# Queries and keys of the block attention as tokens by channels, normed along the row on DVE and turned by PE afterwards

## The reference, cut to what matters

```python
h = rms_norm(x, norm_mix_g[i])
z = h @ w_in[i]
z_glu, gq, gk, gv, gr, ga, mq, mk, mv = jnp.split(z, offsets, axis=-1)
y_a = conformer_conv_branch(z_glu, ...)      # gate, 31 tap convolution, layer norm, silu
y_b = gla_branch(gq, gk, gv, gr, ga, ...)    # gated linear attention, 4 heads
y_c = moba_branch(mq, mk, mv, ...)           # 8 heads of 128 channels

# in moba_branch
q = rms_norm(q.reshape(b_sz, s, MOBA_HEADS, MOBA_HD), q_norm_g).transpose(0, 2, 1, 3)
k = rms_norm(k.reshape(b_sz, s, MOBA_HEADS, MOBA_HD), k_norm_g).transpose(0, 2, 1, 3)
...
s_own = jnp.einsum('bhqd,bhkd->bhqk', qc, k_own).astype(jnp.float32) * scale
```

## Time and profile before

| | us |
|---|---|
| median of 3 runs | 1613.31 (1612.99 to 1614.22) |
| profiled execution, whole | 1614.08 |
| its span, first to last instruction | 1612.0 |
| PE busy | 1596.1 (99%) |
| PE weight loads busy | 1383.0 (86%) |
| DVE busy | 1044.7 (65%) |
| ACT busy | 774.5 (48%) |
| POOL busy | 32.3 (2%) |
| mean granted clock of PE | 0.997 |
| DMA | 297 MB, 184 GB/s |

### The profile page before, as it was taken

The page is one execution under the profiler, slowest core; times in us unless marked ns, Lnnn a source line. Parts: engine busy times, 40 slices in busy tenths (PEclk is TensorE's granted clock), DMA queues, the critical chain, the costliest instruction groups (busy, mean ns, idle before and its releaser), DMA issues.

```text
span 1612.0 us, 23109 instructions
## 1 busy us (share of the span) xinstructions
PE 1596.1 (99%) x8642; PEld 1383.0 (86%) x8642; DVE 1044.7 (65%) x1215; ACT 774.5 (48%) x899; POOL 32.3 (2%) x52
## 2 busy tenths in 40 slices
PE   8999999999999999999999999999999999999998
PEld 7989998888888888888888888888888888888886
DVE  6598655665667646655477777765447777765554
ACT  6444434444555444444455555543345555544543
POOL 5000000000000000000000000000000000000000
PEclk9999999999999999999999999999999999999999
DMA  7666555555655566565566666565665666656564
GB/s 236 178 181 175 165 160 160 172 182 166 196 181 178 184 208 194 184 192 185 162 178 192 189 193 187 182 200 193 191 193 171 194 191 189 193 183 196 175 204 144
DMA packets 155959, 297.23 MB, mean 184 GB/s; under 512 B 9559, under 2 KB 11955, under 8 KB 155888
## 3 DMA queue, kind: packets, MB, share of 16 engines
q1 hardware_dynamic: 155376, 296.00, 59.7%
q0 software_dynamic: 480, 0.25, 0.1%
q10 hardware_dynamic: 32, 0.01, 0.0%
HBM read 294.12 MB, written 2.10 MB: 184 GB/s over the span
## 4 chain that ended last, share of the span: by engine, by line
PE 97%; DVE 1%; DMA 1%; ACT 1%; issue 0%; POOL 0%; SPq 0%; DVEq 0%; ACTq 0%
PE psum L482 20%; PE psum L498 17%; PE psum L500 17%; PE psum L499 17%; PE psum L485 10%; PE psum L461 4%; PE psum L462 4%; PE psum L463 4%; PE psum L578 1%; PE psum L515 1%; PE psum L623 0%; PE psum L532 0%; DMA out<-fin 0%; DVE w_lo L1102 0%; ACT junk L839 0%; DMA xtok<-in_x 0%
## 5 line engine op out<-in xcount | busy, mean ns | idle before, releaser
L1102 DVE TENSOR_TENSOR w_lo<-raw,w_hi 128x1024 fp32r<-128x1024 f32 x550 | 670.2, 1223 | 484.2 <-ACT w_hi L822 483.8
L822 ACT CAST w_hi<-raw 128x1024 fp32r<-128x1024 f32 x550 | 575.4, 1050 | 671.8 <-PE psum L500 409.8
L482 PE MATMUL psum<-h_both,w_hi 128*128 128x512 f32 x1408 | 353.8, 393 | 0.0
L482 PEld LDWEIGHTS psum<-h_both,w_hi 128*128 128x128 f32 x1408 | 254.2, 190 | 45.6
L498 PE MATMUL psum<-w_hi,h_both 128*128 128x512 f32 x608 | 240.5, 396 | 0.4 <-DVE w_lo L1102 0.4
L500 PE MATMUL psum<-w_hi,h_both 128*128 128x512 f32 x608 | 236.9, 390 | 0.0
L499 PE MATMUL psum<-w_lo,h_both 128*128 128x512 f32 x608 | 236.8, 389 | 0.0
L485 PEld LDWEIGHTS psum<-h_both,w_lo 128*128 128x128 f32 x1408 | 192.1, 190 | 13.7
L485 PE MATMUL psum<-h_both,w_lo 128*128 128x256 f32 x1408 | 196.3, 282 | 0.0
L461 PE MATMUL psum<-h_both,w_hi 128*128 128x256 f32 x528 | 151.6, 287 | 3.0 <-DVE h_both L1108 3.0
L462 PE MATMUL psum<-h_both,w_hi 128*128 128x256 f32 x528 | 150.5, 285 | 0.0
(11 more groups left out here) (250 smaller groups left out, 1398.4 us busy)
## 6 DMA issues: line engine op xcount, KB each, us to landing
raw<-in_w_up SPq DMA_DIRECT2D x176, 512.0 KB, 3.7
raw<-in_w_gate SPq DMA_DIRECT2D x96, 512.0 KB, 3.6
raw<-in_w_in SPq DMA_DIRECT2D x90, 512.0 KB, 3.6
raw<-in_w_down SPq DMA_DIRECT2D x88, 512.0 KB, 4.7
raw<-in_w_out SPq DMA_DIRECT2D x32, 512.0 KB, 3.9
raw<-in_w_ple_gate SPq DMA_DIRECT2D x32, 512.0 KB, 4.6
raw<-in_w_moba_out SPq DMA_DIRECT2D x16, 512.0 KB, 3.8
raw<-in_w_conv_out SPq DMA_DIRECT2D x8, 512.0 KB, 3.8
```

The costliest lines, as they stand in the source:

```text
L482: nc.tensor.matmul(wide[part][:, j, :], w_hi[:, c % RING, w], h_both[:, kt + k, :, :].rearrange("p h s -> p (h s)"), start=first and k == ...
L822: A.copy(w_hi[:, c % RING, :], raw[:, c % RING, :]).then_inc(chunk_high, 1)
L1102: V.tensor_tensor(w_lo[:, c % RING, :], raw[:, c % RING, :], w_hi[:, c % RING, :].bitcast(F32), ALU.subtract).then_inc(chunk_split, 1)
```

## The change

The four groups of queries and keys become token chunks. ACT takes a block out as it is, tokens by channels, into `gt` (queries, a tile that the gates use later) or the new tile `ktok` (keys; it lies where `mv` is written later, hence the new wait of the mv take), and squares it into `sqm`. The sum over a head's 128 channels now runs along the row: a tensor_reduce on DVE. Its result is per token on partitions, so keys are multiplied by it on DVE directly, in `ktok`, without a spread. Then PE turns the block in eight transposes into `fa` (`turn_qk`), behind chunk L + 5 for queries and L + 8 for keys, and ACT copies it from there with the norm's gain into `mq` or `mk` at L + 8 and L + 11. The four token_sums and the two spreads of the keys go. DVE's epsilon step comes at L + 8 (queries) and L + 6 (keys), its second step at L + 10 and L + 8. In POOL's list the convolution's power moves behind that of the first keys, and the counts in waits follow.

```diff
+    ktok = ar("ktok", [P, TT, W], 48)
...
-        for k, (cols, first) in enumerate(((8, 0), (TT, STAT_CONV), (8, 0), (8, 0), (8, 0), (8, 0), (TT, 0), (TT, 0))):
+        for k, (cols, first) in enumerate(((8, 0), (8, 0), (TT, STAT_CONV), (8, 0), (8, 0), (8, 0), (TT, 0), (TT, 0))):
...
+        def turn_qk(k):
+
+            if k:
+                pe.wait_ge(qk_taken, k)
+            if k % 2 == 0:
+                wait_taken(pe, NUMBER[("mq", "mq2")[k // 2], 0])
+            else:
+                pe.wait_ge(k_scaled, k // 2 + 1)
+            src = (gt, ktok)[k % 2]
+            dst = turned(0)
+            for j in range(QD):
+                for t in range(TT):
+                    mm = nc.tensor.transpose(dst[:, j, t * P:(t + 1) * P], src[:, t, j * P:(j + 1) * P], ident[:])
+            mm.then_inc(qk_turned, 1)
...
         def scores(h):
             if h == 0:
-                pe.wait_ge(qk_normed, 4)
+                pe.wait_ge(qk_taken, 4)
...
-            if name in ("val", "gate", "qk", "gr", "mq", "mk", "mq2", "mk2"):
+            if name in ("val", "gate", "qk", "gr"):
...
-            elif name in ("gv", "mv", "gA", "gB", "gC"):
+            elif name in ("gv", "mq", "mk", "mq2", "mk2", "mv", "gA", "gB", "gC"):
...
-                spread(3, fb[:, 1, :], 1, STAT_CONV)
+                spread(4, fb[:, 1, :], 1, STAT_CONV)
             for k, name_ in enumerate(("mq", "mk", "mq2", "mk2")):
-                if c == LAST[name_, 0] + 6:
-                    wait_taken(pe, NUMBER[name_, 0])
-                    if k:
-                        pe.wait_ge(qk_normed, k)
-                    token_sums(fa_flat, sqm).then_inc(norm_sums, 1)
-                if c == LAST[name_, 0] + 8 and k % 2:
-                    spread((4, 6)[k // 2], fa_flat, 4)
+                if c == LAST[name_, 0] + (5, 8)[k % 2]:
+                    turn_qk(k)
...
-                    dst = (mq, mk)[k % 2]
-
-                    A.mul(dst[:, 4 * (k // 2):4 * (k // 2) + 4, :], a[:], par[:, R_Q + k % 2:R_Q + k % 2 + 1])
+                    if k >= 2:
+                        act.wait_ge(qk_turned, k - 1)
+                    A.copy((gt, ktok)[k % 2][:], tokens(a))
                     if k:
                         act.wait_ge(norm_sums, k)
                     A.activation(sqm[:], a[:], ACT.Square).then_inc(taken[number % 2], 1)
                 elif name == "mv":
+                    if g == 0:
+                        act.wait_ge(qk_turned, 4)
...
+            for k, name_ in enumerate(("mq", "mk", "mq2", "mk2")):
+                if c == LAST[name_, 0] + (8, 11)[k % 2]:
+                    earlier()
+                    act.wait_ge(qk_turned, k + 1)
+                    A.mul((mq, mk)[k % 2][:, 4 * (k // 2):4 * (k // 2) + 4, :], turned(0),
+                          par[:, R_Q + k % 2:R_Q + k % 2 + 1]).then_inc(qk_taken, 1)
...
-            norm_at[LAST[name_, 0] + 10] = (k, "ms")
-            norm_at[LAST[name_, 0] + 12] = (k, "scale")
+            norm_at[LAST[name_, 0] + (8, 6)[k % 2]] = (k, "ms")
+            norm_at[LAST[name_, 0] + (10, 8)[k % 2]] = (k, "scale")
...
+                by_token = ms[:, 0:8].rearrange("p (h t) -> p t h", t=TT)
                 if what == "ms":
+                    wait_taken(dve, NUMBER[("mq", "mk", "mq2", "mk2")[k], 0])
+                    V.tensor_reduce(by_token, sqm[:].rearrange("p (t a) (b n) -> p t (a b) n", t=TT, n=HD), AX_X, ALU.add).then_inc(norm_sums, 1)
                     dve.wait_ge(norm_sums, k + 1)
-                    V.tensor_scalar(ms[:, 0:8], fa[:, 0, 0:8], 1.0 / HD, EPS, ALU.mult, ALU.add).then_inc(ms_ready, 1)
+                    V.tensor_scalar(ms[:, 0:8], ms[:, 0:8], 1.0 / HD, EPS, ALU.mult, ALU.add).then_inc(ms_ready, 1)
...
-                    dve.wait_ge(rs_spread, (3, 4)[k // 2])
-                    dst = mk[:, 4 * (k // 2):4 * (k // 2) + 4, :]
-                    V.tensor_tensor(dst, dst, fa[:].rearrange("p b (j s) -> p (b j) s", j=2), ALU.mult).then_inc(qk_normed, 1)
+                    dve.wait_ge(rs_ready, (3, 6)[k // 2])
+                    heads = ktok[:].rearrange("p t (h n) -> p t h n", n=HD)
+                    V.tensor_tensor(heads, heads, by_token.unsqueeze(3).broadcast_to([P, TT, 4, HD]), ALU.mult).then_inc(k_scaled, 1)
```

More of the change, by code:

```diff
@@ L256, in trunk @@
     xcsq_folded = sem("xcsq_folded")
-    norm_sums, qk_normed = sem("norm_sums"), sem("qk_normed")
+    norm_sums, k_scaled, qk_turned, qk_taken = (sem(n) for n in ("norm_sums", "k_scaled", "qk_turned", "qk_taken"))
     exps_wanted, exps_ready, level_ready, level_sums, att_ready = (
@@ L1313, in _ @@
                 earlier()
+                by_token = ms[:, 0:8].rearrange("p (h t) -> p t h", t=TT)
                 if what == "ms":
+                    wait_taken(dve, NUMBER[("mq", "mk", "mq2", "mk2")[k], 0])
+                    V.tensor_reduce(by_token, sqm[:].rearrange("p (t a) (b n) -> p t (a b) n", t=TT, n=HD), AX_X, ALU.add).then_inc(norm_sums, 1)
                     dve.wait_ge(norm_sums, k + 1)
-                    V.tensor_scalar(ms[:, 0:8], fa[:, 0, 0:8], 1.0 / HD, EPS, ALU.mult, ALU.add).then_inc(ms_ready, 1)
+                    V.tensor_scalar(ms[:, 0:8], ms[:, 0:8], 1.0 / HD, EPS, ALU.mult, ALU.add).then_inc(ms_ready, 1)
                 elif k % 2 == 0:
                     dve.wait_ge(rs_ready, (2, 5)[k // 2])
-                    V.tensor_scalar(rq[:, k // 2, :], ms[:, 0:8], HD ** -0.5, None, ALU.mult).then_inc(qk_normed, 1)
+                    step(V.tensor_scalar(rq[:, k // 2, :], ms[:, 0:8], HD ** -0.5, None, ALU.mult))
                 else:
-                    dve.wait_ge(rs_spread, (3, 4)[k // 2])
-                    dst = mk[:, 4 * (k // 2):4 * (k // 2) + 4, :]
-                    V.tensor_tensor(dst, dst, fa[:].rearrange("p b (j s) -> p (b j) s", j=2), ALU.mult).then_inc(qk_normed, 1)
+                    dve.wait_ge(rs_ready, (3, 6)[k // 2])
+                    heads = ktok[:].rearrange("p t (h n) -> p t h n", n=HD)
+                    V.tensor_tensor(heads, heads, by_token.unsqueeze(3).broadcast_to([P, TT, 4, HD]), ALU.mult).then_inc(k_scaled, 1)
             if c == CONV_LN + 10:
@@ L1370, in _ @@
                 earlier()
-                dve.wait_ge(rs_spread, 5)
+                dve.wait_ge(rs_spread, 3)
                 dve.wait_ge(gla_r, 1)
@@ L1451, in _ @@
                 earlier()
-                dve.wait_ge(rs_spread, 6)
+                dve.wait_ge(rs_spread, 4)
                 V.tensor_copy(rB[:], fb[:, 0, 0:S]).then_inc(rB_taken, 1)
```

## The result

| | before, us | after, us |
|---|---|---|
| median, 6 runs each, side by side | 1613.15 (1610.90 to 1614.22) | 1600.31 (1598.28 to 1602.15) |
| profiled execution, its span | 1614.08, 1612.0 | 1599.58, 1597.5 |
| PE busy | 1596.1 | 1580.4 |
| DVE busy | 1044.7 | 1049.3 |
| ACT busy | 774.5 | 777.8 |

The ratio is 0.9919, with a 95% interval of 0.9909 to 0.9930: the change makes the kernel 13.1 us faster by the ratio, 12.8 by the two medians, and between 11.3 and 14.7 by the interval. The direction and the terms counted on PE's stream held; the time fell by more than they add up to.

What follows compares the result with a forecast made beforehand. PE's instruction stream, 97% of the span, was taken as the bound. Its terms summed to 12.0 us saved, less waits of 0.7 and 0.2, so 11.1: from 1613.31 to 1602.2 us, range 1600.8 to 1605.0.

Steps and rivals of the forecast that it cites:

- Part 1: Query and key groups: 32 chunks by tokens take 2.728 us each instead of 2.880, saving 4.9 us on PE.
- Parts 2 and 3: Four token_sums and two key factor spreads leave PE, saving 7.05 and 3.6 us.
- Part 4: Four turns of 8 transposes each come onto PE at 0.89 us, adding 3.55 us.
- wait at level 1: PE waits 0.7 us at GLA level 1, as DVE's last key scaling now stands ahead of level_scale.
- wait at level 2: PE waits 0 to 0.6 us at GLA level 2, behind ACT's wait for the fourth turn; 0.2 taken.
- Part 5: ACT's copies behind the turns make casts 2.2 us late, covered by 5.6 us, so they cost PE nothing.
- Part 6: DVE's four reduces, 1.2 to 1.3 us each, and key scalings hide, except for a PE wait at level 1.
- Rivals B and C: B: level 1's wait returns at levels 2 to 8, 1606.4, 0.06; C: each turn costs PE 2.2 us, 1611.0, 0.04.
- E: Token chunks in the query and key groups save nothing on PE; 1607.1 us, chance 0.02.
- D: PE's clock falls at levels 1 to 8 after waits near 3 us; 1644, chance 0.01; milder, at turns, 1611.8, 0.01.
- F: More is saved: no wait at level 1 and turns of 0.79 us; 1600.6 to 1601.5 us, chance 0.03.
- K: Theory from the experiments: in some executions the kernel before pays about 3 us around GLA level 1, the changed one never.

Runs made afterwards that it cites:

- tokens_only: Kernel before with only the 32 query and key chunks as token chunks, the steps behind them unchanged: 1608.69 us, ratio 0.9974.
- take_1: Changed kernel with ACT's copies behind the first three turns one chunk earlier: 1601.88 us, one execution.
- take_2: Changed kernel with ACT's copies behind the first three turns two chunks earlier: 1601.83 us, one execution.
- best: Changed kernel with useless matmuls at PE's two idle places, and the last key scaling one chunk later, behind level_scale 1: 1597.69 us, ratio 0.9903.
- warm_joined: Changed kernel with useless matmuls at PE's two idle places, plus 16 unused one-column matmuls directly before GLA level 1: 1600.99 us, ratio 0.9924.
- two_reduces: Changed kernel with the second keys' reduce done twice, the first into a scratch tile: 1602.36 us, one execution.
- warm_before: Kernel before with useless matmuls at PE's two idle places, the start and the up projection: 1609.79 us, ratio 0.9983.
- warm_apart: Kernel before with useless matmuls at PE's two idle places, and the fourth token_sums one chunk later, away from level 1: 1609.92 us, ratio 0.9978.
- after_again: Changed kernel, unaltered, measured again beside the kernel before: 1601.26 us, ratio 0.9923.
- no_sums: Kernel before without the four token_sums and the two key spreads, nothing in their place: 1601.76 us, ratio 0.9928.

## Why the prediction was right and where it was wrong

Point by point, each term with what it measured, PE's starts of the profiled executions:

| term | forecast, us | measured, us |
|---|---|---|
| Part 1, 32 chunks by tokens | 4.9 | 4.87 (tokens_only: 4.7 in the medians) |
| Parts 2 and 3, sums and spreads | 7.05 + 3.6 | 10.62 |
| Part 4, four turns | 3.55 | 3.57 |
| wait at level 1 | 0.7 | 0.56 |
| wait at level 2 | 0.2 | 0.0 (level 2 costs 1.75 in both) |
| sum | 11.1 | 11.36; whole stretch 11.34 |

**Parts 1 to 4** stood to a tenth of a microsecond, because each was taken from a row of the same form. **Part 5** held: no wait on a weight chunk, and take_1 and take_2 put the edge of the cover between one chunk of delay and two. Only the length of ACT's waits was off: 1 to 1.7 us were announced, the fourth is 2.56. **Part 6** held in kind: the reduce is 1.22, as its nearest row, the tensor_tensor, and not 2.01 as the reduce with 256 outputs; the rule of the Trainium skill ("VectorE: DVE Perf Modes", Rules for kernel authors) had no weight here. And the wait came where it was put, made by the key scaling ahead of level_scale, and best shows that by moving it out of the way. The 0.2 of level 2 did not come. **Rivals B and C** fell: no wait at levels 2 to 8, none on a chunk. **E** fell with tokens_only. **D** is below. **F** went the right way for another reason: its saving on turns and waits did not happen. The time beyond the low end was thus not seen by any rival.

**What failed is the step from the sum to the time: the clock of PE was a term put at nothing, and the spread of the median at 0.3 us.** The prediction subtracted 11.1 from a median, as if all else in both kernels cost the same in every execution. Three things lie in that step.

(a) The terms were 0.26 short: 0.14 at level 1 and 0.20 at level 2, less 0.08 in the rest.

(b) Rival D tied a fall of the clock to a long idle of PE: "Once in this trace it fell", and "It decides from a wait near 3 us; mine are 0.7". The first is a misreading: the trace of before has a second fall, behind the 2.3 us wait at the up projection (0.79 from 784 to 788 us, above). And the runs showed falls with less waiting still: with PE never idle, where one-column matmuls and a level stand together (tokens_only, warm_joined), and with 1.5 us of waiting in two_reduces. The first of these places was in the kernel before and goes with the change: a gain that no row of before's one profile shows, since this profile kept 1.00 there.

(c) Six runs are few where single runs differ by 3.9 us through two clock falls that no change touched; the first six lay 0.8 under the pooled median of eleven, and that pooled median, 1601.07, lies inside the range. Landing outside it is in good part luck. The low end was also tight by the prediction's own terms: 1613.31 less 12.0, less 0.4 for cheap turns, less 0.3 is 1600.6, as rival F has it, and not 1600.8.

Taken together, from 1602.2 to 1600.31: 0.2 is the median of before, 1613.15 with six runs instead of 1613.31 with three; 0.3 are the terms; 0.7 is surplus over the stream, down to the pooled 1601.07; 0.8 is the luck of the first six.

**What stays open.** The surplus is 0.7 us against the six runs of before and 0.9 against all 51 (median 1613.37); by means it is 1.1. K accounts for 0.5 of it by the means of warm_before and warm_apart (1610.42 and 1609.88), which were not taken side by side; their medians, 1609.79 and 1609.92, show nothing of it. Another 0.2 to 0.5 can be a wait for `w_lo` near the end of the program, which the profiles of before, warm_before and warm_apart have (the earlier trace rows has it with 0.4). It is not theirs alone: in after_again a weight load waits at the same place, and the next matmul comes 0.4 us late, though most profiles of the changed family have nothing there:

```profile
1587.39 0.19 PEld L499 LDWEIGHTS psum<-w_hi,h_both 128*128 128x128 f32 x1 [0.57 <-DVE w_lo L1121]
```

No experiment went into it. The split between these and chance isn't settled. Why K's fall comes in some executions and not in others isn't either; only that it did in one profile of tokens_only and one of warm_joined, and not in those of before, warm_before and no_sums (the last has no token_sums at this place).

## What to carry to other kernels

Where PE is the chain, cost an edit by distances between starts of the same form in the same trace; that gave the three terms of the stream to within 0.05 us. Then look for what stands next to what is removed: a cluster of small matmuls can cost a clock fall that the one profile at hand doesn't show, so a single execution's 1.00 is no proof, and the spread of the runs (3.9 us here, 0.15 once the waits were filled) is the sign to look for. And when work leaves PE, ask which producer now comes last at that place: here a reduce and a scaling on DVE cost half a microsecond at one level, and moving the scaling by one chunk gave it back.

## What the runs showed of the chip that was not expected

- The granted clock can fall with PE busy all the time: 4.00 of 4.00 us busy, clock 0.82, then 0.50, behind 16 one-column and 16 64-column matmuls (tokens_only), 0.74 in warm_joined. Steps of a 512 column matmul are 0.427 us then instead of 0.227. With 16 transposes of 128 columns in the same place it stayed at 1.00.
- After a wait it fell behind 1.5 us (two_reduces, 0.60 in the window behind a level) as well as behind 3.0 (0.65, changed kernel at the start; but 1.00 at the same place in two_reduces), and behind the 2.3 us before the up projection in one profile of the changed kernel (after_again, 0.72) but not in the other. The window of after_again:

```profile
774.00:778.00 4.00, 4.00 (x18) 3.54 (x17) 0.16 (x1) 1.05 (x1) 0.00 (x0) 0.72 0.56 217
```

That of the first profile, at the same work:

```profile
770.00:774.00 4.00, 3.87 (x23) 3.48 (x24) 1.69 (x4) 0.31 (x1) 0.00 (x0) 1.00 0.87 280
```

- 22 matmuls without use, put where PE waits, made either kernel 3 to 3.6 us faster (1613.37 to 1609.79, 1601.07 to 1598.07) and the changed one steady to 0.15 us.
- A reduce of 128x1024 costs 1220 ns with 8 outputs per partition, and 2014 with 256.
